# Logits of a head's two maps in turns on the two row halves of the array, and another order of a head's steps

## The chip, the cores and the metric

The kernel runs on one core of a Trainium2 chip. The metric is the time of one execution on the device in microseconds (us). The kernel before takes 2074.48 us, the median of three runs (2073.82 to 2074.49).

Engines in the text: PE is TensorE, DVE is VectorE, ACT is ScalarE, POOL is GpSimd, SP is SyncE. Each has its own queue of instructions and works it off in order; the queues wait for each other by semaphores.

## What is computed

One inference step of two interleaved layers over 128 prompt tokens and 512 latent tokens of width 1024. Layer 0 is a gated linear attention, layer 1 a differential softmax attention, and a SwiGLU FFN follows each. The change lies in the differential attention alone. It has 8 heads with two maps of 64 dimensions each:

```python
def one(qi):
    s = jnp.einsum('bqhcd,bkhcd->bhcqk', qi, k).astype(jnp.float32) * (DIFF_DH ** -0.5)
    p = jax.nn.softmax(s, axis=-1)
    w = p[:, :, 0] - lam * p[:, :, 1]
    return jnp.einsum('bhqk,bkhv->bqhv', w.astype(v.dtype), v)
```

Index c is the map. Latent queries (512) see 256 cached keys and the 512 latent keys, with a rotary embedding on latent queries and keys; prompt queries (128) see the 128 prompt keys only.

## The kernel before

Each engine has one program. All projections are products of a weight tile of 128 x 128 with 640 tokens, in two halves of 320 columns. Every float32 operand is split in a high part and a low part (`w_hi`, `w_lo`; `h_hi`, `h_lo`), and one product is three: high by high, high by low, low by high. ACT makes the high part of the next weights (`split_hi`, L988), DVE the low part (`split_lo`, L1396), PE the products (`tile_products`, L513, L518). A "tile" of a gemm below is one call of `tile_products`, six matmuls.

**The stage of the eight heads.** While PE runs the three gemms of head h (j = 0, 1, 2 for q, k and v, eight tiles each, `dif_gemm`, L935), the attention core of the head before, g, is fitted into the gaps behind their tiles. `core` (L920) is the table: for each gemm, which steps come behind which tile. All three gemms write the accumulator `acc[0]`, so a gemm can start only once ACT has read the unit before (`unit_read`, L1310, copy at L1085).

The steps of a core, by name:

- Rq, Rk: rotation product for queries and keys (`rotate`), AD and AT: a slice of the adaLN product and its turn, VT, KC, KT: transposes of values, cached keys and new prompt keys. They are gaps of the first gemm (`prepare`, L844).
- Sqm: logits of latent query tile q (0 to 3) for map m (`logits`, L869): 128 queries by 768 keys, in 512 and 256 columns, three products each. SP: the same of the prompt tile (q = 4) for both maps (`prompt_logits`, L882).
- T0 to T3, TP: transposes of the combined weights (`w_turn`, L889), six blocks of 128 x 128 for a latent tile, one for the prompt tile.
- O0, O1: values product of tiles 0 and 1, and of 2, 3 and the prompt (`values`, L896). SS: sum of squares of the head's output (`o_squares_sum`, L912).

Between them DVE takes the row maxima (`maxima`, L1804: reduction L1809, negation L1811), the reciprocals (`norms`, L1826), the difference of the two maps (`combine`, L1836) and the low part of the transposed weights (`turned`, L1850). ACT does the exponentials with their row sum (`exps`, L1280), the scale of the first map (`scaled`, L1289), the high part of the transposed weights (`turned`, L1299) and the output's copy (`o_read`, L1305) and squares (L1363). The order on DVE and ACT is written out by hand in each engine's `head` (L1855, L1326).

**Buffers.** The steps use three PSUM buffers in turn: `work`, `side` and `acc[1]`, each of two banks. The step at place n of the list `CORE` uses buffer n modulo 3, and a step waits (`begin`, L816) until the step three places before it in the list has been read. A combined map lives in `w_map[q % 2]` and `p1[q % 2]`; the prompt tile shares number 0 with tiles 0 and 2.

**Queries.** ACT copies the high part of the queries, DVE subtracts the low part, in `operands` (L1248, L1763), for each map its own 64 rows into a padded tile of 128 rows, of which the other 64 are zero (set once by POOL, L476, L477). So a logits product runs over all 128 rows, half of them zeros, with both maps' keys as the other operand.

Order of the steps before, gap by gap (gemm: tile: step): first gemm: 0: Rq, 1: Rk, 2: AD, 3: VT, 4: KC, 5: KT, 6: AT, 7: S00; second: 0: S01, 1: S10, 2: S11, 3: S20, 4: T0, 5: S21, 6: S30, 7: T1; third: 0: S31, 1: O0, 2: SP, 3: T2, 4: T3, 5: TP, 6: O1, 7: SS. After the loop the last head's core runs with no gemm around it.

Of the kernel before, what the change touches and what calls it, by code (L numbers as in the profile page):

```python
# [14 lines left out]
F32 = mybir.dt.float32  # L15
# [5 lines left out]
P = 128  # L21
# [3 lines left out]
T = NS + NP  # L25
# [51 lines left out]
def program(nc, x_prompt, x_sample, state_f, state_b, cache_k, cache_v, c, c_ctx, w_ada, b_ada, g_mix, g_ffn,  # L77
# [3 lines left out]
    with ctx:  # L81
# [114 lines left out]
        q_hi = take("q_hi", [P, 2, T], F32R)  # L196
        q_lo = take("q_lo", [P, 2, T], F32R)
# [61 lines left out]
        dif_in, lam_step, lam_ready, q_zero = sem("dif_in"), sem("lam_step"), sem("lam_ready"), sem("q_zero")  # L259
# [47 lines left out]
        def state_out(d, n):  # L307
            if n >= SCH:
# [5 lines left out]
                "S01", "S10", "S11", "S20", "T0", "S21", "S30", "T1",  # L314
                "S31", "O0", "SP", "T2", "T3", "TP", "O1", "SS"]
# [4 lines left out]
        def buf_of(name):  # L320
            return CORE.index(name) % NB

# [105 lines left out]
        def _(pool):  # L428
# [83 lines left out]
        def _(pe):  # L512
# [356 lines left out]
            def logits(g, q, m):  # L869

                name = f"S{q}{m}"
                out = begin(g, name)
                if q == 0 and m == 0:
                    pe.wait_ge(qs_lo, 2 * g.n + 2)
                    pe.wait_ge(ks_lo, g.n + 1)
                    pe.wait_ge(buf_free[buf_of("KC")], count_of(g, "KC") + 1)
                for a, b in ((0, 512), (512, SK)):
                    mm = split_mul(out[:, a:b], q_hi[:, m, q * P:(q + 1) * P], q_lo[:, m, q * P:(q + 1) * P],
                                   kk_hi[:, a:b], kk_lo[:, a:b])
                mm.then_inc(buf_mm[buf_of(name)], 1)  # L880

            def prompt_logits(g):  # L882
                out = begin(g, "SP")
                for m in range(2):
                    mm = split_mul(out[:, m * P:(m + 1) * P], q_hi[:, m, NS:T], q_lo[:, m, NS:T],
                                   kk_hi[:, SK:SK + P], kk_lo[:, SK:SK + P])
                mm.then_inc(buf_mm[buf_of("SP")], 1)

            def w_turn(g, q):  # L889
                pe.wait_ge(w_ready, NT * g.n + q + 1)  # L890
                if q < 4:
                    turn(g, f"T{q}", [w_map[q % 2][:, t * P:(t + 1) * P] for t in range(SK // P)])
                else:
                    turn(g, "TP", [w_map[0][:, 0:P]])
# [25 lines left out]
            def core(g):  # L920
                def s(q, m):
                    return [lambda: logits(g, q, m)]
# [4 lines left out]
                first[7] = s(0, 0)  # L927
# [1034 lines left out]
```

## Time and profile before

| | us |
|---|---|
| median of 3 runs | 2074.48 |
| lowest, highest | 2073.82, 2074.49 |
| span of the profiled execution | 2074.7 |
| PE busy | 1926.3 |
| DVE busy | 833.7 |
| ACT busy | 718.2 |
| POOL busy | 95.3 |
| mean granted PE clock | 0.972 |

The profile shows one execution. Busy times of different engines overlap; a busy engine isn't the bound for that alone. A matmul's row shows its start, and its length with the pipeline behind it, so what a matmul costs is read from one start to the next. In brackets stands how long the engine had been idle before, and which instruction of which engine ended that.

### The profile page before, as it was taken

To read this page: it belongs to the slowest core of one execution; us is meant where nothing else is said; L and a number is where in the kernel's file an instruction comes from. 1 tells how busy PE (TensorE), PEld (TensorE's weight loads), DVE (VectorE), ACT (ScalarE), POOL (GpSimd) and SP (SyncE) were. 2 spreads that over 40 slices of the span, in tenths; PEclk is the share of its full clock that TensorE was granted. 3 is DMA by queue.
4 is the path that set the end of the run, shared out by engine and by line. 5 is a ranking of instruction groups with operands and counts; after the bars stand their busy time and mean duration, and the time that the engine had idled before them with its cause. 6 is when DMAs were issued, how large, how long until landed. Compare 5 with 4: busy or idle time off the path is not lost.

```text
span 2074.7 us, 29140 instructions
## 1 busy us (share of the span) xinstructions
PE 1926.3 (93%) x11786; PEld 1694.3 (82%) x11786; DVE 833.7 (40%) x1252; ACT 718.2 (35%) x1042; POOL 95.3 (5%) x144
## 2 busy tenths in 40 slices
PE   7899999898999999999899898898597999999997
PEld 2676686667899999999777777777496999999996
DVE  1443343434322323233455555555555223222333
ACT  3624244233422112221545445554535222122222
POOL 1001000010000000000111111001000000000000
PEclk9999999999999999999999999999798999999998
DMA  8233132143222222232322221122021222222221
GB/s 299 71 87 100 54 102 71 44 155 102 82 76 79 84 65 71 71 88 73 100 79 79 69 79 62 39 75 68 3 61 51 71 81 80 72 67 75 79 84 51
DMA packets 227557, 166.00 MB, mean 80 GB/s; under 512 B 7731, under 2 KB 213974, under 8 KB 226470
## 3 DMA queue, kind: packets, MB, share of 16 engines
q1 hardware_dynamic: 213670, 117.21, 19.0%
q0 software_dynamic: 13824, 47.92, 6.9%
q8 instruction: 44, 0.72, 0.1%
q14 instruction: 19, 0.16, 0.0%
HBM read 160.38 MB, written 4.72 MB: 80 GB/s over the span
## 4 chain that ended last, share of the span: by engine, by line
PE 77%; DVE 9%; ACT 8%; issue 5%; DMA 0%; SPq 0%; DVEq 0%; ACTq 0%
PE acc L518 60%; PE side L563 4%; PE side L675 2%; DVE stat L1809 2%; PE work L692 1%; ACT w_hi L988 1%; PE work L612 1%; PE side L612 1%; ACT wt_hi L1299 1%; DVE state L1547 1%; PE work L645 1%; DVE w_map L1836 1%; PE work L689 1%; PE side L826 1%; PE side L825 1%
## 5 line engine op out<-in xcount | busy, mean ns | idle before, releaser
L518 PE MATMUL acc<-h_hi,w_hi 128*128 128x320 f32 x2432 | 589.6, 324 | 43.7 <-DVE h_lo L1453 26.0
L518 PE MATMUL acc<-h_hi,w_lo 128*128 128x320 f32 x2432 | 559.3, 311 | 0.0
L518 PE MATMUL acc<-h_lo,w_hi 128*128 128x320 f32 x2432 | 559.2, 311 | 0.0
L518 PEld LDWEIGHTS acc<-h_hi,w_hi 128*128 128x128 f32 x2432 | 408.7, 191 | 85.6 <-issue 72.7
L1396 DVE TENSOR_TENSOR w_lo<-w_raw,w_hi 128x1024 fp32r<-128x1024 f32 (+1 forms) x184 | 238.1, 1294 | 479.9 <-ACT w_hi L988 479.1
L518 PEld LDWEIGHTS acc<-h_lo,w_hi 128*128 128x128 f32 x2432 | 412.3, 190 | 0.0
L518 PEld LDWEIGHTS acc<-h_hi,w_lo 128*128 128x128 f32 x2432 | 411.4, 190 | 0.0
L988 ACT ACTIVATE w_hi<-w_raw 128x1024 fp32r<-128x1024 f32 (+1 forms) x184 | 204.0, 1109 | 441.5 <-PE acc L518 441.5
L518 PE MATMUL acc<-hid_lo,w_hi 128*128 128x320 f32 x704 | 160.4, 309 | 0.0
L518 PE MATMUL acc<-hid_hi,w_lo 128*128 128x320 f32 x704 | 160.4, 309 | 0.0
L518 PE MATMUL acc<-hid_hi,w_hi 128*128 128x320 f32 x704 | 160.4, 309 | 0.0
L1198 ACT ACTIVATE hid_hi<-hid_f 128x640 f32 (+1 forms) x44 | 32.5, 739 | 269.0 <-DVE hid_f L1677 269.0
L518 PEld LDWEIGHTS acc<-hid_hi,w_lo 128*128 128x128 f32 x704 | 117.7, 188 | 0.0
L518 PEld LDWEIGHTS acc<-hid_hi,w_hi 128*128 128x128 f32 x704 | 117.7, 188 | 0.0
L518 PEld LDWEIGHTS acc<-hid_lo,w_hi 128*128 128x128 f32 x704 | 117.7, 188 | 0.0
L1677 DVE TENSOR_TENSOR hid_f<-silu_g,acc 128x640 f32<-128x640 f32 x44 | 36.1, 821 | 199.7 <-PE acc L518 198.1
L1645 DVE SCALAR_TENSOR_TENSOR x<-acc,mods,x 128x320 f32<-128x320 f32 x144 | 54.3, 433 | 109.1 <-PE acc L518 109.1
L563 PE MATMUL side<-a_raw,cond 128*2 128x512 f32 x192 | 91.5, 612 | 3.6 <-DVE mods L1460 3.6
L437 POOL DMA_DIRECT2D a_raw<-in_w_ada_dram x52 | 37.8, 727 | 706.4 <-PE side L563 678.4
L1000 ACT ACTIVATE sq<-x 128x640 f32<-128x640 f32 x35 | 25.8, 738 | 119.6 <-DVE x L1645 119.4
L563 PEld LDWEIGHTS side<-a_raw,cond 128*2 128x2 f32 x192 | 13.6, 85 | 56.9 <-issue 52.7
L1547 DVE SCALAR_TENSOR_TENSOR state<-state,decay,side 128x256 f32<-128x256 f32 x64 | 30.7, 480 | 67.6 <-PE side L675 65.1
(282 smaller groups left out, 1967.3 us busy)
## 6 DMA issues: line engine op xcount, KB each, us to landing
a_raw<-in_w_ada_dram POOLq DMA_DIRECT2D x80, 512.0 KB, 5.1
w_raw<-in_w_ffn_gate_dram SPq DMA_DIRECT2D x44, 512.0 KB, 3.8
w_raw<-in_w_ffn_up_dram SPq DMA_DIRECT2D x44, 512.0 KB, 3.8
w_raw<-in_w_ffn_down_dram SPq DMA_DIRECT2D x32, 704.0 KB, 4.6
w_raw<-in_w_gla_in_dram SPq DMA_DIRECT2D x24, 512.0 KB, 3.9
w_raw<-in_w_diff_qkv_dram SPq DMA_DIRECT2D x24, 512.0 KB, 3.9
a_first_h<-in_w_ada_dram SPq DMA_DIRECT2D x5, 1024.0 KB, 12.0
w_raw<-in_w_gla_out_dram SPq DMA_DIRECT2D x8, 512.0 KB, 4.0
```

The source lines that it names most:

```text
L437: pool.dma_start(a_raw[q][:, :, :], wl[:, 2 * q:2 * q + 2, bass.ds(b % AB * 512, 512)])\
L518: mm = pe.matmul(out[:, s, 0:HALF], w[slot][:, k * P:(k + 1) * P], a(k)[:, s * HALF:(s + 1) * HALF], start=(k == 0 and n == 0), stop=(k == ...
L563: mm = pe.matmul(out[0:2, 0:512], cond[:, 2 * q + j, :], a_raw[q][:, j, :], start=(q == 0 and j == 0), stop=(q == 3 and j == 1))
L612: mm = pe.matmul(first_rows[b], cond[:, k, :], a_first(k)[:, b * 512:(b + 1) * 512], start=(k == 0), stop=(k == KD - 1))
L675: mm = pe.matmul(spare[:, i % 2, :], k_end[:, n // 2, n % 2, :], v_tok[:, n // 2, :], start=True, stop=True)
L988: act.activation(w_hi[slot][:, 0:kt * P], w_raw[slot][:, 0:kt * P], ACT.Copy).then_inc(hi_ready, 1)
L1198: act.activation(hid_hi[:, bass.ds(i, 1), :].rearrange("p a n -> p (a n)"), hid_f[:, :], ACT.Copy).then_inc(hidh_ready, 1)
L1396: dve.tensor_tensor(w_lo[slot][:, 0:kt * P], w_raw[slot][:, 0:kt * P], w_hi[slot][:, 0:kt * P].bitcast(F32), ALU.subtract).then_inc(lo_rea ...
L1547: dve.scalar_tensor_tensor(out=state_out(d, n), in0=before, scalar=decay[:, d, n:n + 1], in1=spare[:, i % 2, :], op0=ALU.mult, op1=ALU.add)\
L1645: op = dve.scalar_tensor_tensor(out=xk[:, lo:hi], in0=acc[slot][:, half, lo - half * HALF:hi - half * HALF], scalar=mods[:, one, v], in1=x ...
L1677: dve.tensor_tensor(hid_f[:, :].rearrange("p (s n) -> p s n", s=2), silu_g[:, :].rearrange("p (s n) -> p s n", s=2), acc[1][:, :, 0:HALF], ...
L1809: dve.tensor_reduce(stat[:, q, m:m + 1], out[:, 0:SK], AX_X, ALU.max).then_inc(mx_done, 1)
```

## The change

- Queries are no longer padded. `q_hi` and `q_lo` hold both maps, 64 rows each, in one tile, copied and subtracted in one instruction each. POOL's four zero fills and the semaphore for them go.
- A logits step makes both maps of a query tile. The products of the maps take turns: map 0 on rows 0 to 63 of the array, map 1 on rows 64 to 127, each into its own buffer (for the prompt tile, each into its own bank of one buffer). The step begins only when both buffers are free.
- The prompt tile has maps of its own (`w_mapp`, `p1p`) and is second in a head (`TILES`), after tile 0. `CORE`, and so the buffer of each step, PE's gaps, and the order on ACT and DVE follow.

Order of the steps after: first gemm as before up to 6, then 7: S0 (both maps); second: 0: SP, 2: S1, 4: T0, 5: TP, 6: S2; third: 0: T1, 1: S3, 3: O0, 4: T2, 5: T3, 6: O1, 7: SS. Tiles 1, 3, 7 of the second gemm and 2 of the third have nothing behind them.

```diff
-        q_hi = take("q_hi", [P, 2, T], F32R)
-        q_lo = take("q_lo", [P, 2, T], F32R)
+        q_hi = take("q_hi", [P, T], F32R)
+        q_lo = take("q_lo", [P, T], F32R)
+        w_mapp, p1p = take("w_mapp", [P, P]), take("p1p", [P, P])
...
         CORE = ["Rq", "Rk", "AD", "VT", "KC", "KT", "AT", "S00",
-                "S01", "S10", "S11", "S20", "T0", "S21", "S30", "T1",
-                "S31", "O0", "SP", "T2", "T3", "TP", "O1", "SS"]
+                "S01", "SP", "S10", "S11", "T0", "TP", "S20", "S21",
+                "T1", "S30", "S31", "O0", "T2", "T3", "O1", "SS"]
+        TILES = [0, 4, 1, 2, 3]
...
-            for t in (q_hi, q_lo):
-                pool.memset(t[CH:P, 0, :].bitcast(F32), 0.0).then_inc(q_zero, 1)
-                pool.memset(t[0:CH, 1, :].bitcast(F32), 0.0).then_inc(q_zero, 1)
...
+            def map_products(outs, cols, keys, g, names=None):
+
+                for n, (qq, kk) in enumerate(((q_hi, kk_hi), (q_hi, kk_lo), (q_lo, kk_hi))):
+                    for m in range(2):
+                        rows = slice(m * DH, (m + 1) * DH)
+                        mm = pe.matmul(outs[m], qq[rows, cols], kk[rows, keys], start=(n == 0), stop=(n == 2))
+                        if names and n == 2:
+                            mm.then_inc(buf_mm[buf_of(names[m])], 1)
+                return mm
+
+            def logits(g, q):
+
+                names = [f"S{q}{m}" for m in range(2)]
+                outs = [begin(g, name) for name in names]
...
                 for a, b in ((0, 512), (512, SK)):
+                    map_products([out[:, a:b] for out in outs], slice(q * P, (q + 1) * P), slice(a, b), g,
+                                 names if b == SK else None)
...
-                        {0: s(0, 1), 1: s(1, 0), 2: s(1, 1), 3: s(2, 0), 4: t(0), 5: s(2, 1), 6: s(3, 0), 7: t(1)},
-                        {0: s(3, 1), 1: [lambda: values(g, 0)], 2: [lambda: prompt_logits(g)], 3: t(2), 4: t(3),
-                         5: t(4), 6: [lambda: values(g, 1)], 7: [lambda: o_squares_sum(g)]}]
+                        {0: [lambda: prompt_logits(g)], 2: s(1), 4: t(0), 5: t(4), 6: s(2)},
+                        {0: t(1), 1: s(3), 3: [lambda: values(g, 0)], 4: t(2), 5: t(3), 6: [lambda: values(g, 1)],
+                         7: [lambda: o_squares_sum(g)]}]
...
-                for m in range(2):
-                    rows = slice(m * DH, (m + 1) * DH)
-                    act.activation(q_hi[rows, m, :], q_f[rows, :], ACT.Copy).then_inc(qs_hi, 1)
+                act.activation(q_hi[:, :], q_f[:, :], ACT.Copy).then_inc(qs_hi, 1)
...
                 exps(g, 0, 0)
                 exps(g, 0, 1)
+                exps(g, 4, 0)
+                exps(g, 4, 1)
+                scaled(g, 0)
                 exps(g, 1, 0)
-                scaled(g, 0)
+                scaled(g, 4)
                 exps(g, 1, 1)
                 scaled(g, 1)
                 turned(g, 0)
+                turned(g, 4)
                 exps(g, 2, 0)
                 exps(g, 2, 1)
                 if h:
...
                 exps(g, 3, 0)
                 exps(g, 3, 1)
+                scaled(g, 3)
                 o_read(g, 0)
-                scaled(g, 3)
                 turned(g, 2)
-                exps(g, 4, 0)
-                exps(g, 4, 1)
                 turned(g, 3)
-                scaled(g, 4)
-                turned(g, 4)
...
                 maxima(g, 0, 0)
                 maxima(g, 0, 1)
+                maxima(g, 4, 0)
+                norms(g, 0)
                 maxima(g, 1, 0)
-                norms(g, 0)
+                norms(g, 4)
                 combine(g, 0)
                 maxima(g, 1, 1)
+                combine(g, 4)
                 norms(g, 1)
+                turned(g, 0)
+                turned(g, 4)
+                combine(g, 1)
                 maxima(g, 2, 0)
-                combine(g, 1)
-                turned(g, 0)
                 maxima(g, 2, 1)
-                maxima(g, 3, 0)
                 norms(g, 2)
                 turned(g, 1)
                 if h:
                     next_split(h, 2)
                 combine(g, 2)
+                maxima(g, 3, 0)
                 maxima(g, 3, 1)
                 norms(g, 3)
-                maxima(g, 4, 0)
                 combine(g, 3)
                 turned(g, 2)
-                norms(g, 4)
                 turned(g, 3)
-                combine(g, 4)
-                turned(g, 4)
```

## Rows read from the trace of the kernel before

**Rows 1.** The page: busy time of the engines and their share of the span

```profile
PE 1926.3 (93%) x11786; PEld 1694.3 (82%) x11786; DVE 833.7 (40%) x1252; ACT 718.2 (35%) x1042; POOL 95.3 (5%) x144
```

**Rows 2.** Stretches: length, busy PE, PEld, DVE, ACT, POOL; PE clock, DMA share, GB/s

```profile
1209.20:1267.50 58.30, 52.53 (x302) 42.42 (x302) 34.70 (x61) 29.65 (x52) 5.45 (x8) 0.97 0.22 70
1230.40:1233.70 3.30, 3.30 (x13) 3.01 (x12) 0.29 (x2) 1.65 (x2) 3.30 (x6) 0.50 0.49 125
...
1476.50:1479.50 3.00, 2.54 (x7) 1.96 (x8) 2.96 (x6) 2.50 (x4) 0.00 (x0) 0.50 0.00 0
```

**Rows 3.** Timeline of PE over one head: start, length, line, out<-in [idle before <-releaser]

```profile
1209.49 1.31 PE L917 MATMUL acc<-o_sqr,ones 128*128 128x320 f32 x4 [0.58 <-ACT o_sqr L1363]
...
1229.12 1.05 PE L574 MATMUL work<-ident,a_row 2*128 2x2 f32 x8 [2.42 <-DVE vv_lo L1787]
...
1231.65 0.63 PE L825 MATMUL side<-kk_hi,q_hi 128*128 128x512 f32 x1
...
1236.47 0.39 PE L825 MATMUL work<-kk_hi,q_hi 128*128 128x512 f32 x1
...
1237.51 0.46 PE L518 MATMUL acc<-h_hi,w_hi 128*128 128x320 f32 x2
...
1238.39 0.39 PE L825 MATMUL side<-kk_hi,q_hi 128*128 128x512 f32 x1
...
1249.92 0.53 PE L518 MATMUL acc<-h_hi,w_hi 128*128 128x320 f32 x2 [0.43 <-ACT k_f L1085]
...
1262.63 0.32 PE L841 MATMUL work<-ident,w_map 128*128 128x128 f32 x1 [1.35 <-DVE w_map L1836]
...
1263.67 0.28 PE L825 MATMUL side<-wt_hi,vv_hi 128*128 128x256 f32 x1
...
1267.78 1.31 PE L917 MATMUL acc<-o_sqr,ones 128*128 128x320 f32 x4 [0.58 <-ACT o_sqr L1363]
```

**Rows 4.** Timeline of DVE in that head: the first row maximum

```profile
1234.72 0.95 DVE L1809 TENSOR_REDUCE stat<-side 128x1 f32<-128x768 f32 x1
```

**Rows 5.** DVE in that head, grouped: shapes, count, busy us, mean ns, idle before

```profile
L1836 DVE SCALAR_TENSOR_TENSOR w_map<-p,stat,w_map 128x768 f32<-128x768 f32 x4 | 4.1, 1019 | 1.6 <-ACT w_map L1289 1.6
L1809 DVE TENSOR_REDUCE stat<-side 128x1 f32<-128x768 f32 x4 | 3.8, 950 | 0.0
L1396 DVE TENSOR_TENSOR w_lo<-w_raw,w_hi 128x1024 fp32r<-128x1024 f32 x3 | 3.7, 1221 | 3.0 <-ACT w_hi L988 3.0
...
L1850 DVE TENSOR_TENSOR wt_lo<-work,wt_hi 128x768 fp32r<-128x768 f32 x2 | 1.9, 956 | 1.8 <-ACT wt_hi L1299 1.8
L1771 DVE TENSOR_TENSOR q_lo<-q_f,q_hi 64x640 fp32r<-64x640 f32 x2 | 1.6, 821 | 0.8 <-ACT q_hi L1257 0.8
```

**Rows 6.** ACT in that head, grouped in the same way

```profile
L1289 ACT ACTIVATE w_map<-w_map,stat 128x768 f32<-128x768 f32 x4 | 3.7, 933 | 0.2 <-DVE stat L1826 0.2
L988 ACT ACTIVATE w_hi<-w_raw 128x1024 fp32r<-128x1024 f32 x3 | 3.2, 1054 | 0.0
L1280 ACT ACTIVATE p<-side,stat 128x768 f32<-128x768 f32 x3 | 2.7, 903 | 6.1 <-DVE stat L1811 6.1
...
L1299 ACT ACTIVATE wt_hi<-work 128x768 fp32r<-128x768 f32 x2 | 1.6, 802 | 0.0
...
L1085 ACT ACTIVATE k_f<-acc 128x640 f32<-128x640 f32 x1 | 0.7, 693 | 0.0
```

**Rows 7.** Timeline of PE in layer 0: products into column halves (128*64) between full ones

```profile
164.99 1.08 PE L692 MATMUL work<-state,q_d 128*64 128x256 f32 x8
166.00 0.70 PE L689 MATMUL work<-v_tok,attn 128*128 128x256 f32 x2
166.63 1.08 PE L692 MATMUL work<-state,q_d 128*64 128x256 f32 x8
```

**Rows 8.** Timeline of PE: two of the six prompt logits products

```profile
1256.67 0.27 PE L827 MATMUL work<-kk_hi,q_lo 128*128 128x128 f32 x1
1256.78 0.27 PE L825 MATMUL work<-kk_hi,q_hi 128*128 128x128 f32 x1
```

More of the change, by code:

```diff
@@ L867, in prepare @@
                         3: [v_turn], 4: [k_turn], 5: [lambda: turn(g, "KT", [k_f[:, NS:T]])], 6: [ada_columns]}
[L869 to L874, printed above, removed]
+            def map_products(outs, cols, keys, g, names=None):
[9 more added lines that the diff above has]
+                outs = [begin(g, name) for name in names]
+                if q == 0:
+                    pe.wait_ge(qs_lo, g.n + 1)
                     pe.wait_ge(ks_lo, g.n + 1)
@@ L893, in w_turn @@
                 else:
-                    turn(g, "TP", [w_map[0][:, 0:P]])
+                    turn(g, "TP", [w_mapp[:, :]])
             def values(g, pp):
@@ L962, in _ @@
                 for k in range(KD):
-                    for f in gaps[k]:
+                    for f in gaps.get(k, ()):
                         f()
@@ L1271, in exps @@
             def exps(g, q, m):
-                i = 2 * (NT * g.n + q) + m
+                i = 2 * tile_no(g, q) + m
                 act.wait_ge(nm_ready, i + 1)
-                if m == 1 and not (g.first and q < 2):
-                    act.wait_ge(w_ready, NT * g.n + q - 1)
+                if m == 1:
+                    if q >= 2 and q < 4:
+                        act.wait_ge(w_ready, tile_no(g, q - 2) + 1)
+                    elif not g.first:
+                        act.wait_ge(w_ready, tile_no(g.before(), q + 2 if q < 2 else q) + 1)
                 name = f"S{q}{m}" if q < 4 else "SP"
                 n = SK if q < 4 else P
-                src = bufs[buf_of(name)][:, 0:n] if q < 4 else bufs[buf_of(name)][:, m * P:(m + 1) * P]
-                op = act.activation((w_map, p1)[m][q % 2][:, 0:n], src, ACT.Exp, bias=stat[:, q, 2 + m:3 + m], scale=DH ** -0.5,
+                src = bufs[buf_of(name)][:, 0:n] if q < 4 else buf2[buf_of(name)][:, m, 0:P]
+                op = act.activation(maps_of(q)[m][:, 0:n], src, ACT.Exp, bias=stat[:, q, 2 + m:3 + m], scale=DH ** -0.5,
                                     accum_out=stat[:, q, 4 + m:5 + m])
@@ L1765, in operands @@
                 rope(g, 0, "Rq", q_f)
-                for m in range(2):
-                    rows = slice(m * DH, (m + 1) * DH)
-                    dve.wait_ge(qs_hi, 2 * g.n + m + 1)
-                    if g.first:
-                        dve.wait_ge(q_zero, 4)
-                    dve.tensor_tensor(q_lo[rows, m, :], q_f[rows, :], q_hi[rows, m, :].bitcast(F32), ALU.subtract)\
-                        .then_inc(qs_lo, 1)
+                dve.wait_ge(qs_hi, g.n + 1)
+                dve.tensor_tensor(q_lo[:, :], q_f[:, :], q_hi[:, :].bitcast(F32), ALU.subtract).then_inc(qs_lo, 1)
                 rope(g, 1, "Rk", k_f)
```

53 lines of the change are left out of this document (26 added, 27 removed).

## The prediction

> **What bounds the kernel now.** I read the engine totals first: TensorE is busy for 93% of the span [rows 1]. This is an average over stages with different limits, so I then cut out the stage that the change touches, the eight heads of the differential attention. The SS product of one head starts at 1209.49, that of the next at 1267.78 [rows 3]: 58.29 us a head. In that stretch TensorE is busy 52.5, DVE 34.7, ACT 29.7 us [rows 2]. TensorE looks like the bound, but six times a head it stands still for another engine; the three that matter here are 2.42 us before the AT product (for DVE's vv_lo), 0.43 before the third gemm (for ACT's k_f) and 1.35 before the prompt turn (for DVE's w_map) [rows 3]. Between the first logits and the second values product the steps form one long chain PE, DVE, ACT, DVE, PE through three PSUM buffers, and the gemm tiles (eight per gemm, three gemms) are what TensorE does while it waits for the chain. The question is therefore what happens to that chain, not only how many columns TensorE saves.
>
> **Prices.** A block of logits for one map takes 1236.47 to 1237.51 = 1.04 us, a gemm tile 1237.51 to 1238.39 = 0.88 us [rows 3]. Six transposes take about 0.57 from start to start and 0.28 more to be readable (from the timeline of the same head; the two terms weigh little). DVE: row maximum 0.95 and its small negation, together 1.07 until the next can start; combine 1.02, wt_lo 0.95, w_lo 1.22 [rows 5]. ACT: exponential 0.90 with its accumulator read, 1.0 together; scale 0.93, wt_hi 0.80, k_f 0.69, w_hi 1.05 [rows 6].
>
> **Part 1: queries not padded.** ACT copied q_hi in two halves of 64 rows and DVE subtracted in two, 0.82 each [rows 5]; a half costs what a whole does, since the columns are the same 640. One subtraction disappears: 0.84 us with its start. From there the chain of the first stage runs on unbroken (rotate keys, kk_hi, inverse root, Newton steps, o_buf, vv_lo) to the AT product, which waits 2.42 us [rows 3]. So AT starts 0.84 earlier; 1.58 of the wait remains. Late next is the same vv_lo. In the very first head the chain has no Newton steps and AT waits for other things: gain nothing there. GpSimd's four memsets go; they lie ahead of its first load of cached keys, before the first head, and nobody waits for them: nothing.
>
> **Part 2: two maps in turns on the row halves.** Before, two maps cost 2.08 us. The trace before has no half-row products; the nearest is the GLA output, where products into two column halves alternate [rows 7]: eight products of 256 columns take 164.99 to 166.00 = 1.01 us, while two full products of the same width behind them take until 166.63, 0.63 us. If all ran in line, eight would cost four times two, 1.5 to 2.5 us; so the halves do run side by side. As four side-by-side steps (1.01) and two full ones (0.63), a step is 0.19 and 0.25 is left over at a change of form. For the row halves: each product still loads 128 columns of weights, and the prompt products show that loads limit: with only 128 columns they follow at 0.11 us [rows 8], a quarter of the columns of a latent product. Twelve loads of 0.11 are 1.33; two changes of up to 0.25 bring 1.33 to 1.83, and I take 1.7 for a pair, a saving of 0.38. Ends: 1.04 (full overlap, loads too, free changes) and 2.4 (no overlap, two changes). The prompt's six products are load-limited before and after: 0.65 becomes 1.0.
> The Trainium skill, "TensorEngine Tiling (Array Packing)", Key Properties, says that a change of tiling mode drains TensorE; [rows 7] agree in kind (up to 0.25 us); without it a pair would be 1.33. "TensorE: Matmul & The Clock Gate", LDWEIGHTS, says that a load's time goes by its columns, not its rows; no row here has a 64-row load.
>
> **Part 3: the order.** This is the large part. CORE is permuted, so the buffers of a step and its predecessor change: S20, S21 now sit in buffers 2 and 0, and buffer 0 was last used by T0. Both maps are issued together, so S2 as a whole waits until DVE's wt_lo of T0 has read it. Walk, on the clock of [rows 3], without Part 1:
> S0 starts at 1231.65 (half clock, see below) and ends by 1234.3; DVE can't begin its maximum before 1234.72 anyway [rows 4], because w_lo lies ahead of it. Maxima 00 and 01 end at 1236.9, the prompt's (0.6) at 1237.6; exponential 01 ends 1.1 behind its maximum, at 1238.0, and frees buffer 2. TensorE, with tile, prompt, two tiles, is there at 1238.0. S1: 1238.15 to 1239.85, readable at 1240.05.
> From there in series: maximum 10 (1.07), norms of the prompt tile (0.28), combine 0 (0.94), maximum 11 (1.12), exponential 11 (1.0), its reciprocal (0.23), scale 1 (0.84), wt_hi 0 (0.79), wt_lo 0 (0.95), and 0.2 of semaphores: 7.4, so S2 can start at 1247.4. TensorE does tiles 3 and 4 until 1241.65, waits 0.8 for combine 0, does T0, tile 5, TP and tile 6 and is done at 1245.0: a new wait of 2.4 us. Behind it are queued tile 7 and everything of the third gemm.
> S2: until 1249.1, readable 1249.3; two maxima 2.2, exponential 21 1.05, then k_f 0.65, which stands behind it in ACT's queue: the third gemm can start at 1253.2. Before it started at 1249.92 [rows 3], so 3.3 us later. TensorE waits 3.2 us there in place of 0.43.
> Then in series: tile 0 (0.9), T1 (0.57 and 0.28 to be readable), wt_hi 1 (0.71), w_hi of the next unit (1.05), w_lo (1.2; DVE has it ahead of combine 2), combine 2 (0.94), maxima 30, 31 (2.2), exponential 31 (1.05), reciprocal (0.23), scale 3 (0.94), combine 3 (1.1), T3 (0.82), wt_hi 3 (0.8), wt_lo 3 (1.05): 13.9, second values product at 1267.15 in place of 1263.67 [rows 3]. The prompt turn's wait of 1.35 is gone, but nothing is won by that, since T3 is now late. From values to SS are 4.11 us as before. So a head is 3.48 longer, and with Part 1 2.64 longer.
>
> **The clock.** Once a head, after the 2.42 us before AT, the granted clock falls to 0.50 (1.2 of 2.4 GHz) for 3.4 us [rows 2]; in the last head, where TensorE has no gemm tiles to do between its waits, it is at 0.50 again from 1476.5 to 1479.5 [rows 2]. The two new waits are as long as the one before AT. A fall behind the first doubles S2 (+1.0 at most), one behind the second tile 0 and T1 (+1.2); a fall that no longer comes behind AT gives back 0.7. At chances of 0.4, 0.5 and 0.6: +0.4 +0.6 -0.4 = +0.6 a head. Bounds -0.7 and +2.2.
>
> **Sum.** Seven heads with gemms 7 x 3.48 = 24.4; Part 1 in six of them -5.0; the last head has no gemm to delay and no k_f or w_hi in the chain: between 0 and 3.5, I take 2.2 with Part 1 in it; clock 7 x 0.6 = 4.2. Together +25.8 on the profiled execution, whose span of 2074.7 is within 0.3 us of the runs' median of 2074.48: 2100.5.
>
> **Rivals.**
> Full overlap (chance 0.14): a pair costs 1.04. S1 and S2 are both on the chain and S3 is not (combine 2 is later), so 2 x 0.66 = 1.3 less per head, 10.5 in all: 2090. For it the short steps of [rows 7]; against it the loads of [rows 8].
> TensorE bounds, and the time follows its work (chance 0.11), faster: four pairs at 1.04 saved less 0.35 for the prompt, 1.35 of the prompt turn's wait, 0.84 of AT: 4 x 1.04 - 0.35 + 1.35 + 0.84 = 6.0 a head, 2027; with loads limiting, 3.4 a head, 2048. For it the 93%. Against it that the buffers tie S2 to wt_lo 0. The skill's "TensorEngine Tiling (Array Packing)", Theoretical Speedup, gives up to 2x for 64 rows, which is this case's 1.04.
> The products don't overlap at all (chance 0.08), the change doesn't do what it says: 2.2 to 2.4 a pair, +0.6 at two places: +1.1 a head, 2109.
> The clock falls behind both new waits in every head (chance 0.13): +2.2 in place of +0.6, 2112; with slow pairs 2119.
> The two orders cancel (chance 0.05): if exponential 21 and k_f were not in series behind S2, the third gemm would start 2.5 earlier, within 1 us of before: about 2077. It decides at 0.6 us a head (4.1 us in all).
> The forecast itself, with a load-limited pair and the new waits, 0.49.
> Slower, one mechanism: S2 tied to wt_lo of T0; it decides from the moment when TensorE runs out of tiles, at 1245.0, which is 2.4 us too early.
>
> **How the numbers follow.** Predicted 2100.5. The range takes in full overlap without any falls (2084) and falls in every head (2118): 2084 to 2118; outside lie the faster case and the cancelling one, and extremes of others. About 0.2% is what a measurement of this kernel can tell from no change (4.1 us): faster 0.12, same 0.06, slower 0.82.
>
> **What would show it.** SS to SS near 61 us; a wait before the first product of S2 (releaser DVE wt_lo) of about 2 us; a wait of about 3 us before the third gemm for ACT k_f; no wait before the prompt turn; AT's wait near 1.6; two maps' products starting together, and a pair from 1.3 to 1.7. It would be wrong if S2 finds its buffers free, if a pair's loads go side by side, or if the third gemm starts within 1 us of its old place.

## The result, and the profile after

The changed kernel takes 2098.97 us (median, 2097.12 to 2102.25) against 2074.32 us of the kernel before, run beside it on the same chip: a ratio of 1.0114, with a 95% interval of 1.0102 to 1.0127. It is slower by 24.7 us; 2100.5 was forecast. The profiled execution has a span of 2097.8 us, 23.1 more than before.

The page of the profile after, its first lines:

```profile
span 2097.8 us, 29138 instructions
PE 1918.7 (91%) x11786; PEld 1681.0 (80%) x11786; DVE 827.7 (39%) x1244; ACT 714.7 (34%) x1034; POOL 92.8 (4%) x140
```

Every engine is busy for less time than in [rows 1], and the kernel is slower: what grew is idle time, and the time at the lower clock. The same view by heads as in [rows 2], from SS to SS (columns: stretch, its length, busy us and instructions of PE, PEld, DVE, ACT and POOL, granted clock, DMA share, GB/s), and then one stretch inside the second of them:

```profile
1155.60:1216.10 60.50, 51.15 (x303) 40.04 (x303) 34.02 (x60) 29.36 (x51) 5.45 (x8) 0.94 0.22 68
1216.10:1277.80 61.70, 53.22 (x302) 41.62 (x303) 34.01 (x60) 29.27 (x51) 5.45 (x8) 0.89 0.21 66
1253.30:1263.40 10.10, 7.96 (x34) 6.97 (x32) 3.86 (x9) 5.16 (x8) 0.00 (x0) 0.50 0.00 0
```

A head that took 58.3 us takes 60.5 or 61.7, and its clock, 0.97 in [rows 2], is 0.94 or 0.89. TensorE's timeline of the head from 1216.09, which answers to [rows 3] (start, length, operation; in brackets the idle time before it and who ended that):

```profile
1216.09 1.31 PE L931 MATMUL acc<-o_sqr,ones 128*128 128x320 f32 x4 [0.58 <-ACT o_sqr L1377]
...
1234.74 1.05 PE L580 MATMUL work<-ident,a_row 2*128 2x2 f32 x8 [1.44 <-DVE vv_lo L1796]
...
1240.58 0.33 PE L880 MATMUL work<-kk_hi,q_hi 64*128 64x128 f32 x2
...
1241.06 0.56 PE L524 MATMUL acc<-h_hi,w_hi 128*128 128x320 f32 x2
...
1243.67 0.47 PE L880 MATMUL side<-kk_hi,q_hi 64*128 64x512 f32 x1 [0.58 <-ACT p L1293]
1243.67 0.49 PE L880 MATMUL acc<-kk_hi,q_hi 64*128 64x512 f32 x1
...
1244.91 0.56 PE L524 MATMUL acc<-h_hi,w_hi 128*128 128x320 f32 x2
...
1252.42 0.49 PE L880 MATMUL acc<-kk_hi,q_hi 64*128 64x512 f32 x1 [2.19 <-DVE wt_lo L1859]
...
1258.13 0.87 PE L524 MATMUL acc<-h_hi,w_hi 128*128 128x320 f32 x2 [2.14 <-ACT k_f L1099]
...
1273.62 0.38 PE L831 MATMUL side<-wt_hi,vv_hi 128*128 128x256 f32 x1 [1.02 <-DVE wt_lo L1859]
...
1277.81 1.31 PE L931 MATMUL acc<-o_sqr,ones 128*128 128x320 f32 x4 [0.58 <-ACT o_sqr L1377]
```

Read it from the top. The AT product (L580) waits 1.44 us in place of 2.42. The prompt's two maps (L880, `64x128`) take 1240.58 to 1241.06 = 0.48. Then a pair of maps, S1: its first products, one into `side` and one into `acc`, start in the same hundredth, and the next gemm tile starts at 1244.91, so a pair costs 1.24 us, where two maps one after the other cost 2.08. At 1252.42 stands the first new wait, S2 for DVE's wt_lo, 2.19 us; at 1258.13 the second, the third gemm for ACT's k_f, 2.14 us. The waits of TensorE over six heads (line, releaser, total us, times, longest), before:

```profile
PE work L574 <- DVE vv_lo L1787: 14.5, 6, 2.4
PE work L841 <- DVE w_map L1836: 8.1, 6, 1.4
PE acc L825 <- ACT w_map L1280: 6.0, 12, 0.6
PE acc L917 <- ACT o_sqr L1363: 3.5, 6, 0.6
PE acc L518 <- ACT k_f L1085: 2.3, 6, 0.4
```

and after:

```profile
PE acc L524 <- ACT k_f L1099: 13.4, 6, 3.0
PE acc L880 <- DVE wt_lo L1859: 13.2, 6, 2.2
PE work L580 <- DVE vv_lo L1796: 8.6, 6, 1.5
PE side L831 <- DVE wt_lo L1859: 6.1, 6, 1.0
PE work L847 <- DVE w_map L1845: 4.3, 8, 0.9
PE side L880 <- ACT p L1293: 3.7, 5, 1.5
PE acc L931 <- ACT o_sqr L1377: 3.5, 6, 0.6
```

The sums are 34.4 and 52.8 us, 5.7 and 8.8 a head: 3.1 us more idle time. TensorE's busy time, by the windows of the same six heads, falls only from 53.0 to 52.1 a head, though every pair is 0.84 us cheaper at the full clock. Idle 3.1 more, busy 0.9 less: 2.2 us a head, which is what the six heads show (365.7 against 352.7 us, 13.1 in all).

Where the 23.1 us lie: 3.85 up to the first SS (1091.46, now 1095.31), 13.1 in the six heads, 3.6 in the last head, which has no gemm (55.0, now 58.6), 2.6 behind it. The 3.85 are two things. The first rotation product starts at 1038.1 in place of 1039.35, and from there to the first SS it takes 57.2 us in place of 52.1: the first head with gemms costs 5.1, and 1.25 came back ahead of it. The code ahead of it is the same but for POOL's fills. Over the fourteen profiled kernels of this text this first rotation product starts between 1036.6 and 1041.2 us, and the part behind the last SS takes 575.4 to 578.3 us, so a difference of a few us in these two parts says nothing about the heads.

### The profile page after: what moved, and what is told of

Its sections match the earlier page's. It is cut to its first block, busy times and chain, and to the rows that moved or that the text cites. A ratio compares the mean times of both kernels' runs of the same rounds, so it can differ in the third digit from the quotient of the medians.

```text
span 2097.8 us, 29138 instructions
## 1 busy us (share of the span) xinstructions
PE 1918.7 (91%) x11786; PEld 1681.0 (80%) x11786; DVE 827.7 (39%) x1244; ACT 714.7 (34%) x1034; POOL 92.8 (4%) x140
## 4 chain that ended last, share of the span: by engine, by line
PE 79%; DVE 9%; ACT 7%; issue 4%; DMA 0%; SPq 0%; ACTq 0%; DVEq 0%
PE acc L524 60%; PE side L569 4%; DVE stat L1818 2%; PE acc L569 2%; PE side L681 2%; PE acc L880 1%; PE work L698 1%; ACT p L1293 1%; ACT w_hi L1002 1%; DVE wt_lo L1859 1%; PE work L618 1%; ACT wt_hi L1313 1%; PE side L880 1%; PE side L618 1%; DVE state L1561 1%
## 5 line engine op out<-in xcount | busy, mean ns | idle before, releaser
L524 PE MATMUL acc<-h_hi,w_hi 128*128 128x320 f32 x2432 | 596.9, 327 | 57.5 <-DVE h_lo L1467 26.1
L1014 ACT ACTIVATE sq<-x 128x640 f32<-128x640 f32 x35 | 25.8, 738 | 119.7 <-DVE x L1659 119.4
```

The lines of the kernel that those rows point to most:

```text
L524: mm = pe.matmul(out[:, s, 0:HALF], w[slot][:, k * P:(k + 1) * P], a(k)[:, s * HALF:(s + 1) * HALF], start=(k == 0 and n == 0), stop=(k == ...
```

## The experiments

Time is the median of the kernel beside the kernel before on the same chip; the ratio is to that, with its 95% interval.

### The order alone, and the products alone

**e1_padded** keeps the changed order and takes the row halves away: padded queries, and a map's three products in line.

```diff
-                for n, (qq, kk) in enumerate(((q_hi, kk_hi), (q_hi, kk_lo), (q_lo, kk_hi))):
-                    for m in range(2):
-                        rows = slice(m * DH, (m + 1) * DH)
-                        mm = pe.matmul(outs[m], qq[rows, cols], kk[rows, keys], start=(n == 0), stop=(n == 2))
+                for m in range(2):
+                    for n, (qq, kk) in enumerate(((q_hi, kk_hi), (q_hi, kk_lo), (q_lo, kk_hi))):
+                        mm = pe.matmul(outs[m], qq[:, m, cols], kk[:, keys], start=(n == 0), stop=(n == 2))
```

> The changed kernel's order of steps, with the queries padded again and full-array products, one map after the other (Parts 1 and 2 undone, Part 3 alone). If the order is what costs and the row halves are a gain, this is slower than the changed kernel: a pair goes from 1.24 us (measured there) to about 2.08, and two pairs a head (S1 and S2) lie on the chain, so +1.7, and the AT wait is longer by 0.84: about +2.5 us a head, 2115 to 2120. If the row form itself is what costs, this falls back towards the time of before, 2075 to 2085.

Measured: 2130.69 us, 1.0268 (1.0251 to 1.0285). The order costs more than expected, 56 us. Its heads come in kinds; two neighbours by the windows view:

```profile
1291.50:1354.50 63.00, 52.67 (x302) 42.32 (x302) 34.87 (x61) 29.72 (x52) 5.45 (x8) 0.97 0.21 65
1354.50:1420.80 66.30, 56.84 (x303) 46.14 (x303) 35.00 (x61) 29.98 (x52) 5.46 (x8) 0.90 0.20 61
```

With the clock at 0.97, as before, a head takes 63.0 us. The walk of the prediction gives 62.5 for it (58.29 + 3.48, and 2 x 0.38 because S1 and S2 are on the chain at 2.08 in place of 1.7). So the walk holds to 0.5 us where the clock does not fall more often; in the heads at 0.90, 3 us come on top. The one fall of that head comes with the wait for k_f and not behind AT, so the two aren't quite alike. The waits stand at the same two places as in the kernel after (2.2 us before S2, up to 2.8 before the third gemm).

**e2_old_order_rows** is the other half: the order of before, queries not padded, each map alone on its 64 rows, no two of them together.

```diff
-                    mm = split_mul(out[:, a:b], q_hi[:, m, q * P:(q + 1) * P], q_lo[:, m, q * P:(q + 1) * P],
-                                   kk_hi[:, a:b], kk_lo[:, a:b])
+                    rows = slice(m * DH, (m + 1) * DH)
+                    mm = split_mul(out[:, a:b], q_hi[rows, q * P:(q + 1) * P], q_lo[rows, q * P:(q + 1) * P],
+                                   kk_hi[rows, a:b], kk_lo[rows, a:b])
```

> The order, buffers and steps of the kernel before, with unpadded queries and each map's products on its own 64 rows, so never two maps side by side (Part 1 alone, with the change of form at each block). If the split of the queries gives its 0.84 us a head and a change of form costs 0.1 to 0.25 at blocks that mostly hide, the time is 2068 to 2073. If the row form costs by itself, 2080 or more. A block of one map should take 1.04 us plus a change of form.

Measured: 2129.7 us, 1.0263 (1.0246 to 1.028): slower by 55 us, where a small gain or nothing was expected. AT's wait is 1.45 us, so Part 1 does what was forecast. The loss is the clock, in the windows view:

```profile
1246.50:1269.00 22.50, 22.50 (x70) 18.53 (x71) 9.21 (x17) 8.02 (x13) 3.64 (x6) 0.50 0.41 129
```

For 22.5 us TensorE is busy without a gap, and the granted clock is 0.50 (1.2 GHz); in the six heads such a stretch lasts 20.5 to 23.9 us. In [rows 2] a fall lasts 3.4 us. This was a surprise, and the next runs follow it further below.

### Which wait costs what

**e3_kf_first** is meant to loosen the second wait: S2 behind tile 7 of the second gemm, and ACT copies k_f ahead of the exponentials of tile 2. The tile that S2 now stands behind also fills a part of the first wait.

```diff
-4: t(0), 5: t(4), 6: s(2)},
+4: t(0), 5: t(4), 7: s(2)},
...
+                if h:
+                    unit_read(h, 1)
                 exps(g, 2, 0)
                 exps(g, 2, 1)
-                if h:
-                    unit_read(h, 1)
```

> The changed kernel with S2 behind tile 7 of the second gemm instead of tile 6, and ACT's copy of k_f ahead of the exponentials of tile 2 instead of behind them. The third gemm then waits for neither. If k_f's place in ACT's queue costs what the walk said, the wait of about 2.1 to 3.0 us before the third gemm goes, T1 comes some 2.5 to 3 us earlier and the time is 2078 to 2084. If only the tie of S2 to T0's buffer counts and the rest would be late anyway, it stays at 2095 to 2100.

Measured: 2075.98 us, 1.0002 (0.9992 to 1.0012). Moving one copy ahead of two exponentials, and one step by a tile, is worth 23 us. The wait for k_f is gone; S2 still waits for wt_lo, 1.3 us in place of 2.2, and the turns wait up to 1.6 for w_map. Each of the six heads has one fall of the clock, behind AT, where the kernel after has two or three or a longer one, so a part of the 23 us is clock; how much belongs to the copy and how much to the step isn't shown. The gain of the row halves is now just eaten by what is left of the order.

**e4_s2_before_t0** unties S2 from wt_lo of T0 as well: S2 comes ahead of T0 and TP in CORE, so it takes buffers that are long free, and ACT and DVE follow. ACT's copy of k_f stands ahead of the exponentials as in e3, and DVE's w_lo of the next unit goes behind the maxima of tile 3.

```diff
-                "S01", "SP", "S10", "S11", "T0", "TP", "S20", "S21",
+                "S01", "SP", "S10", "S11", "S20", "S21", "T0", "TP",
...
-                        {0: [lambda: prompt_logits(g)], 2: s(1), 4: t(0), 5: t(4), 6: s(2)},
-                        {0: t(1), 1: s(3), 3: [lambda: values(g, 0)],
+                        {0: [lambda: prompt_logits(g)], 2: s(1), 5: s(2), 6: t(0)},
+                        {0: t(4), 1: t(1), 2: s(3), 3: [lambda: values(g, 0)],
```

> The changed kernel with S2 ahead of T0 and TP, in the buffer list, in TensorE's gaps and on ACT and DVE, so that its buffers are those of SP and S10 and not that of T0, and with k_f ahead of the exponentials of tile 2. Both new waits should go. If the order is the whole loss and the paired products are a gain, a head gets shorter than before, to about 53 to 55 us, and the time is 2040 to 2055. If the loss has another source, it stays at 2090 to 2100.

Measured: 2044.12 us, 0.9854 (0.9837 to 0.987). TensorE's waits over six heads:

```profile
PE work L580 <- DVE vv_lo L1796: 8.7, 6, 1.5
PE side L831 <- DVE wt_lo L1859: 6.1, 6, 1.0
PE acc L524 <- ACT k_f L1099: 6.0, 6, 1.1
PE side L880 <- ACT p L1293: 5.0, 4, 1.5
PE acc L931 <- ACT o_sqr L1377: 3.5, 6, 0.6
```

The wait of S2 is gone and that for k_f is 1.0 in place of 2.2 a head. The sum is 29.3, which is 3.9 us a head less than in the kernel after; a head is 7.1 us shorter (323.3 against 365.7 us for six). The rest is busy time, 49.0 us a head in place of 52.1, by the clock: 0.94 to 1.00 in these heads, three of the six at 1.00, where the kernel after has 0.89 to 0.94. The edit moves several steps at once, and how the 32 us from e3 to e4 divide among them isn't shown.

**e7_s2_before_t0_padded** is e4 with the padded queries and the products in line, as in e1.

> The order with S2 ahead of T0 (which took 2044), with queries padded and full-array products in line, as before. It prices the paired products and the single query split in an order that is good for them. With 0.84 us more in each of four pairs, 0.2 for the prompt and the second half's subtraction (0.84), and some of it hidden: +2.5 to +4.4 us a head, 2064 to 2080. If the pairs are worth nothing, 2044 to 2050.

Measured: 2074.12 us, 0.9997 (0.9988 to 1.0007). This closes a square:

| | padded, in line | row halves, both maps together |
|---|---|---|
| order of e4 | 2074.1 (e7) | 2044.1 (e4) |
| order of the change | 2130.7 (e1) | 2099.0 (after) |

Both maps together, with Part 1, win 30.0 or 31.7 us; the order of the change loses 56.6 or 54.9. The order of e4, padded, is as fast as the order of before. So the change is -32 and +56. How the -32 divides between Part 1 and the pairs no run shows by itself; AT starts 0.9 us earlier in each head of e4 than in e7, so an estimate for Part 1 is 6 x 0.9, some 5 us.

### Do the halves need the turns?

**e6_not_in_turns** issues the three products of map 0, then the three of map 1.

```diff
-                for n, (qq, kk) in enumerate(((q_hi, kk_hi), (q_hi, kk_lo), (q_lo, kk_hi))):
-                    for m in range(2):
-                        rows = slice(m * DH, (m + 1) * DH)
+                for m in range(2):
+                    rows = slice(m * DH, (m + 1) * DH)
+                    for n, (qq, kk) in enumerate(((q_hi, kk_hi), (q_hi, kk_lo), (q_lo, kk_hi))):
```

> The changed kernel with the three products of map 0 issued first and then those of map 1, on the same row halves. If products overlap only with their neighbour in the queue, a pair takes 1.24 us no longer but 1.9 to 2.3 us, and, since half-row products alone went with a clock of 0.50 for over 20 us in a head when they were never paired, the time is 2115 to 2145. If the order within a pair doesn't matter, it stays at 2099.

Measured: 2099.32 us, 1.0105 (1.0087 to 1.0122), the time of the kernel after. Of the two cases of the expectation the second holds; the range 2115 to 2145 of the first was missed. TensorE's timeline, S1 of a head:

```profile
1246.53 0.50 PE L880 MATMUL side<-kk_hi,q_hi 64*128 64x512 f32 x1
1246.54 0.50 PE L880 MATMUL acc<-kk_hi,q_hi 64*128 64x512 f32 x1
...
1247.79 0.56 PE L524 MATMUL acc<-h_hi,w_hi 128*128 128x320 f32 x2
```

The first product of map 1 is issued fourth and starts 0.01 us behind the first of map 0; the pair takes 1.26 us. So in groups of three the halves run side by side without turns.

**e10_one_half_at_a_time** forbids it: e4, but map 1's products wait until map 0's have ended. The prompt's maps stay side by side.

```diff
+                for m in range(2):
+                    rows = slice(m * DH, (m + 1) * DH)
+                    for a, b in ((0, 512), (512, SK)):
+                        mm = split_mul(outs[m][:, a:b], q_hi[rows, q * P:(q + 1) * P], q_lo[rows, q * P:(q + 1) * P],
+                                       kk_hi[rows, a:b], kk_lo[rows, a:b])
+                    mm.then_inc(buf_mm[buf_of(names[m])], 1)
+                    if m == 0:
+                        pe.wait_ge(buf_mm[buf_of(names[0])], count_of(g, names[0]) + 1)
```

> The order with S2 ahead of T0 (2044), with the latent logits of map 1 held until those of map 0 have ended, so that only one row half works at a time (the prompt's stay as they are). TensorE's time at full clock is close to that of the padded form in this order (2074, which also holds 0.84 us for the second subtraction): a pair of 2.08 plus some 0.4 for the wait and the changes of form. If half the array at work counts like the whole for the granted clock, the time is 2068 to 2085. If the clock stays at 0.50 while half the array works, as in the run with the old order, 2095 to 2130, with a mean clock near 0.94 in place of 0.97.

Measured: 2095.78 us, 1.0098 (1.0081 to 1.0115). Side by side is worth 51.7 us here (e4 has 2044.1), and half-row products in line are worse than padded ones in line by 21.7 us (e7). Part of it is the wait between the maps (a pair takes about 2.8 us); part is the clock, low for 9.8 us at a time with TensorE hardly ever idle:

```profile
1236.90:1246.70 9.80, 9.74 (x36) 8.05 (x34) 4.17 (x9) 4.77 (x11) 3.32 (x5) 0.50 0.92 287
```

### The clock

**e5_fill** fills both new waits of the changed kernel with eight products of 512 columns each, whose results nobody reads.

```diff
+            def fill(out, n):
+                for _ in range(n):
+                    mm = pe.matmul(out[:, 0:512], kk_hi[:, 0:P], kk_hi[:, 0:512], start=True, stop=True)
+                return mm
...
+                if q == 2:
+                    fill(begin(g, "S20"), 8)
...
+                if j == 2 and not (isinstance(h.i, int) and h.n == 0):
+                    fill(begin(h.before(), "T1"), 8)
```

> The changed kernel with eight extra full-array products of 512 columns (about 1.85 us) in each of its two new waits, before S2 (into the buffer that S20 overwrites) and before the third gemm (into the buffer that T1 overwrites). They add work and free nothing; only the granted clock can gain. If the falls to 0.50 behind those waits cost 1 to 1.8 us a head, as the profile of the changed kernel suggests (T1's way in the head from 1216 to 1278 took 3.2 us in place of 1.75), the clock stays near 1 there, S2 and the third gemm start no later, and the time is 2086 to 2094. If the falls are hidden behind ACT and DVE, it stays at 2097 to 2102.

Measured: 2088.01 us, 1.0061 (1.0044 to 1.0078). More work, 11 us less. **e8_fill_half** fills with 64 rows only, to see whether work on half the rows counts as work for the clock:

```diff
-                    mm = pe.matmul(out[:, 0:512], kk_hi[:, 0:P], kk_hi[:, 0:512], start=True, stop=True)
+                    mm = pe.matmul(out[:, 0:512], kk_hi[0:DH, 0:P], kk_hi[0:DH, 0:512], start=True, stop=True)
```

> As the run with the waits filled, but the filling products use 64 rows only. If the granted clock depends on how much of the array works and not only on whether TensorE is busy, the clock still falls behind these waits, the filling runs at half speed and delays S2 and the third gemm, and the time is 2098 to 2125. If only busy time counts, it is that of the run with full products, 2086 to 2094.

Measured: 2092.07 us, 1.0079 (1.0062 to 1.0096). One head of each, e5 and then e8:

```profile
1214.00:1273.40 59.40, 51.97 (x318) 40.28 (x318) 33.98 (x60) 29.17 (x51) 5.44 (x8) 1.00 0.22 68
```

```profile
1217.64:1277.05 59.41, 52.32 (x319) 40.23 (x319) 33.97 (x60) 29.18 (x51) 5.45 (x8) 1.00 0.22 68
```

They are as long as each other. The 3.7 us between the two profiled executions lie elsewhere: the first rotation product already starts 3.7 us later in e8, ahead of any fill. From there to the first SS it takes 57.2 us in place of 55.8, and there the clock falls in e8 right behind the half-row fill before the third gemm:

```profile
1079.00:1082.00 3.00, 3.00 (x14) 2.96 (x14) 0.00 (x0) 0.46 (x2) 0.00 (x0) 0.50 0.02 5
```

In e5 it is at 1.00 in this place. Over the seven heads with gemms, no fall comes behind any of the 14 waits that full rows fill, and one behind the 14 that half the rows fill; the kernel after has 12. So fills of half the rows, some 1.9 us long, hold the clock nearly as full ones do, and the case of the expectation in which they would not (2098 or more) fell. What holds it low in e2 and e10 is more than "half the rows for a moment".

### A version that beats both

**e9_at_behind_7** is e4 with the AT product one tile later, behind tile 7 of the first gemm and just ahead of S0, so that the tile fills the wait for vv_lo.

```diff
-5: [lambda: turn(g, "KT", [k_f[:, NS:T]])], 6: [ada_columns]}
+5: [lambda: turn(g, "KT", [k_f[:, NS:T]])], 7: [ada_columns]}
...
-first[7] = s(0)
+first[7] = first[7] + s(0)
```

> The order with S2 ahead of T0 (2044), and the AT product behind tile 7 of the first gemm instead of tile 6, so that one tile (0.88 us) fills its wait of 1.45 us. If that wait is on the path, a head gets 0.9 us shorter and, where the clock no longer falls behind it, up to 0.7 more: 2033 to 2039. If the chain over DVE's vv_lo sets the start of the maxima anyway, nothing changes: 2042 to 2046.

Measured: 2027.58 us (2026.32 to 2028.56), 0.9771 (0.9754 to 0.9787), the fastest of all and below the 2033 to 2039 that were expected. A head:

```profile
1188.80:1240.00 51.20, 47.82 (x302) 37.48 (x302) 33.73 (x60) 29.16 (x51) 5.44 (x8) 1.00 0.25 79
```

AT waits 0.6 us, and none of the six heads from SS to SS has a fall: all are at 1.00 and take 51.1 to 51.3 us. But e4 has three heads at 1.00 too, and they take 53.5 to 53.6. So the move wins 2.4 us a head with no clock in it, where AT's wait shrank by 0.9 alone. ACT and DVE show the rest, in the head of e4 that begins at 1086.62:

```profile
1107.44 0.70 ACT L1099 ACTIVATE q_f<-acc 128x640 f32<-128x640 f32 x1 [5.04 <-PE acc L524]
1109.12 1.22 DVE L1410 TENSOR_TENSOR w_lo<-w_raw,w_hi 128x1024 fp32r<-128x1024 f32 x1 [2.35 <-ACT w_hi L1002]
1110.26 0.95 DVE L1818 TENSOR_REDUCE stat<-side 128x1 f32<-128x768 f32 x1
```

and in the head of e9 that begins at 1086.42:

```profile
1104.55 0.70 ACT L1099 ACTIVATE q_f<-acc 128x640 f32<-128x640 f32 x1 [2.36 <-PE acc L524]
1106.53 1.23 DVE L1410 TENSOR_TENSOR w_lo<-w_raw,w_hi 128x1024 fp32r<-128x1024 f32 x1
1107.67 0.95 DVE L1818 TENSOR_REDUCE stat<-side 128x1 f32<-128x768 f32 x1
```

With AT ahead of tile 7, the last tile of the first gemm stands behind AT's wait, and behind that tile stand in series ACT's copy of q_f, w_hi, DVE's w_lo and, behind w_lo in DVE's queue, the first row maximum. With AT behind tile 7 that whole series is out of the way, and the first maximum starts 21.3 us behind SS in place of 23.6.

**e12_before_at7** makes this one move in the kernel before.

> The kernel before with the AT product behind tile 7 of the first gemm instead of tile 6, nothing else. One tile fills 0.88 us of the 2.42 us wait. If wait and clock are on the path, a head gains 0.9 us and, where the clock doesn't fall, up to 1.5 more: 2058 to 2068. If the chain over vv_lo and w_lo sets the start of the maxima, 2072 to 2076.

Measured: 2062.94 us, 0.9936 (0.992 to 0.9953), as expected: 13 us for one move. AT's wait falls from 2.4 to 1.5 us, and its heads take 55.8 us at 1.00 or 57.4 at 0.97: three of each in six. Here the clock does count: a head with the fall is 0.9 us shorter than the 58.3 of before, by the one tile, and a head without it 2.4.

**e11_rows_at7** makes it in e2, so that the AT wait which precedes e2's long stretch at 1.2 GHz shrinks to 0.58 us.

> The old order with each map alone on its 64 rows (2129.7), and the AT product behind tile 7 instead of tile 6. In that kernel the clock fell to 0.50 behind the wait for AT and stayed there for over 20 us. If half-row products alone only fail to bring the clock back, and the wait is what makes it fall, it no longer falls and the time is 2065 to 2085. If half-row products make it fall by themselves, the time stays at 2105 to 2130.

Measured: 2105.0 us (2097.41 to 2107.88), 1.0147 (1.013 to 1.0164), far above the first case and at the lower end of the second; two of its four runs lie below 2105. Two kinds of head:

```profile
1155.20:1220.40 65.20, 62.48 (x303) 48.52 (x303) 34.15 (x60) 29.24 (x51) 5.44 (x8) 0.84 0.20 63
1350.90:1407.00 56.10, 53.35 (x303) 41.16 (x303) 33.80 (x60) 29.12 (x51) 5.46 (x8) 1.00 0.23 72
```

Without a fall the head is 56.1 us long, no longer than e12's by more than 0.3. With one it is 9.1 longer, as the clock stays at 0.50 for some 20 us. The fall begins behind a wait of 0.58 us in four of the six heads and not in the other two. Whether the half-row products themselves start it stays open, and so does the part of AT, whose eight tiny products (1.05 us) stand between the wait and them in every head; that it lasts six times as long with them than in [rows 2] is measured.

## Why the prediction was right

The time was 1.5 us off, but this is closer than the terms were, and that part is luck: the pair of maps was priced 6.4 us too dear over the seven heads, the last head and what is behind it 4.0 too cheap. What wasn't luck is the order: the two waits, their releasers and their places. On the profiled execution the forecast is 2.7 us too high. The sum again, on the profiled execution, with each term as measured:

| term | forecast | measured |
|---|---|---|
| ahead of the first rotation product | 0 | -1.25 |
| walk: first gemm head 3.48, six heads at 2.64 | +19.3 | +12.9, an estimate, by the pair below |
| clock in these seven | +4.2 | +5.3 (what is left of 18.2) |
| last head | +2.2 | +3.6 |
| behind the last head | 0 | +2.6 |
| sum | +25.8 | +23.1 |

**Part 1: right.** AT's wait is 1.44 (forecast 1.58); the four memsets cost and give nothing that is seen.

**Part 2: the step "loads limit" failed.** A pair was put at 1.7 from the spacing of [rows 8] times twelve loads; it takes 1.24, and the prompt's six products 0.48 in place of 1.0. TensorE's weight loads of S1, in the kernel after, show why:

```profile
1243.64 0.18 PEld L880 LDWEIGHTS side<-kk_hi,q_hi 64*128 64x128 f32 x1 [0.81 <-issue]
1243.67 0.18 PEld L880 LDWEIGHTS acc<-kk_hi,q_hi 64*128 64x128 f32 x1
```

The loads of the two halves run side by side too, so twelve loads cost what six do. The prediction named this as what would prove it wrong. With 1.24, S1 and S2 bring 2 x 0.46 = 0.92 less a head, 6.4 in seven: 19.3 becomes 12.9. What is above the full overlap of 1.04 is 0.20 a pair: about 0.1 for each of the two changes of form, if they share it, below the 0.25 read from [rows 7]. "TensorEngine Tiling (Array Packing)" of the Trainium skill, Theoretical Speedup, allows up to 2x; measured are 2.08 / 1.24 = 1.7.

**Part 3: right, place by place.** From SS on, with the 0.84 of Part 1 off:

| | forecast | measured |
|---|---|---|
| S1 starts | 27.8 | 27.6 |
| S2 starts | 37.1, wait 2.4 | 36.3, wait 2.2 |
| third gemm starts | 42.9, wait 3.2 | 42.0, wait 2.1 here, up to 3.0 |
| wait before TP | none | none |
| second values product | 56.8 | 57.5 |
| next SS | 60.9 and clock | 61.7 |

Both waits have the releasers that were named, wt_lo and k_f. The first three rows are early by about what the pairs were over-priced. From the third gemm to the values it is 15.5 us where the walk has 13.9: the stretch from 1253.3 to 1263.4, shown above, is at 1.2 GHz. That the two waits are the cause and not only there in the trace is shown by e3 (the second off, the first shorter: 23 us less) and e4 (both loosened: 55 less).

**The clock: the sum near, its parts not.** Falls were given chances of 0.4 and 0.5 behind the new waits and 0.6 for the one behind AT to vanish. By the granted clock over the six heads there is one behind S2's wait in five of six, behind k_f's in six of six (in two heads run together with that before), and behind AT still in five; some 58 us at 0.50 in all, where before has 27. That should have cost far more than 0.6 a head. It did not, since before is no clean base: in two of its six heads the fall behind AT lasts 7 us, so that they take 59.7 and 59.8 in place of 58.3 (their mean is 58.8), and because work at half clock is partly hidden ahead of the next wait. The walk has one short fall behind AT in it. With the pair at 1.24 it gives 58.29 + 2.64 - 0.92 = 60.0, and e5's three heads with that fall alone take 59.8 to 59.9. Against 60.0, the further falls cost a head of the kernel after 1.0 us (61.0), and the longer ones cost a head of before 0.5 (58.8): a net of 0.5, where 0.6 was forecast. The first head with gemms, which has no fall in the kernel before, has one now, and costs 5.1 us for 3.5 of the walk. The price of the fall behind AT, 0.7 a head, was too small for the old order and too large for the new one: with and without it a head of e12 takes 57.4 and 55.8, a head of e5 59.9 and 59.4.

**The last head and the end: undersized, and missed.** The last head has no gemm to delay, but the new order lengthens its chain by 3.6 us, above the bound of 3.5. Behind it, 2.6 us: the SS product there takes 2.47 us at the lower clock in place of 1.32, and over the 100 us that begin 75 us behind it the clock is 0.92 where before has 0.94. This part of the kernel was taken as untouched, and its code is; what reached it is the clock. It takes 575.4 to 578.3 us in the profiled kernels, so the 2.6 us are within what it varies by, and the same holds for the 1.25 us ahead of the first head.

**The rivals.** Full overlap was nearly right about the pair (1.24 lies nearer to 1.04 than to 1.7), and gave 2090. Falls behind both waits was nearly right about the falls (11 of 12), and gave 2112. They miss to opposite sides, and the forecast lay between. "The two orders cancel" was 2077 under the condition that k_f is not in series behind S2's exponentials; e3 makes that condition true, and moves S2 besides, and takes 2076.0. The agreement is in part chance: by the prediction's own terms the rival comes to 7 x (3.48 - 2.5) - 5.0 + 2.2 + 4.2 = 8.3 us more than before, 2083; 2077 leaves out the last head and the clock. "TensorE bounds" was 2027 to 2048; with the buffers untied it is 2044.1 (e4). That e9 takes 2027.6 is no proof of its lower end, since the move of AT isn't in that sum. Between faster and slower the order decided, as the prediction said.

## What to carry to other kernels

Price a new tiling and the new order that comes with it apart: here the first wins 30 to 32 us and the second loses 55 to 57, and the order could be had without the loss by putting the step that needs two buffers at once (S2) ahead of the step that uses one of them (T0). A step that takes both buffers is released by the later of the two, so walk the chain to its last reader; and look at what stands in an in-order queue behind it (k_f behind two exponentials; that copy and one step moved by a tile, 23 us). When a tile is moved into a wait, count what stands behind the tile as well: one move won 13 us in the kernel before and 16.5 in e4, where AT's own waits in six heads shrank by 5 each time. In the kernel before, the clock gave the rest; in e4, for the most part, the last tile of the gemm released a copy, a split and with them DVE's queue 2.4 us earlier.

## What the runs showed of the hardware

- Products on the two 64-row halves ran side by side, loads included, in turns or in groups of three (e6, 2099.3 against 2099.0). A pair of maps took 1.24 us against 2.08 in line; six prompt products 0.48 against 0.62 (in [rows 3]'s head, 1256.50 to 1257.12).
- Half-row products in line are not free against padded ones: 2129.7 against 2074.3 in the order of before (e2), 2095.8 against 2074.1 in that of e4 (e10, with a wait between the maps). With them, in the heads with gemms, a fall of the clock to 1.2 GHz lasted 10 to 24 us with TensorE hardly ever idle; with full rows, or with both halves at work, 3.4 to 10.2 us, mostly 3.4. In the last head, with its many waits, falls are long with full rows too (23.9 us in e1). Part 1 alone, with each map on its own 64 rows, would have been a loss of 55 us. In a wait, though, 1.9 us of half-row work held the clock up in 13 of 14 waits (e8), full rows in 14 of 14 (e5). What sets these apart was not found.
- Falls came behind waits of 2.2 us and of 0.6 us (e11), and in some heads not behind the same wait. The same head of the same kernel thus has two or three lengths (e12: 55.8 and 57.4; e1: 63.1, 64.2 and 65.9 to 66.2). The same fall costs what the order lets it: 1.5 us a head in e12, 0.4 in e5.
